# Eight experts' products in native float32 on four column tiles, with 96 token slots and a weight ring that is read as it lands

## The reference

```python
def moe_swiglu(v, router, wg, wu, wd):          # v: 256 x 1024
    logits = (v @ router).astype(F32)           # 8 experts
    top_val, top_idx = lax.top_k(logits, 2)
    top_w = jax.nn.softmax(top_val, axis=-1)
    combine = jnp.sum(jax.nn.one_hot(top_idx, 8, dtype=F32) * top_w[..., None], axis=-2)
    y = jnp.zeros_like(v)
    for e in range(8):                          # wg, wu: 1024 x 2816, wd: 2816 x 1024
        y = y + combine[..., e:e + 1] * swiglu(v, wg[e], wu[e], wd[e])
    return y
```

## Time and profile before

| | |
|---|---|
| time, median of 3 runs | 1569.23 us (1567.52 to 1570.71) |
| the profiled execution | 1568.84 us, its span 1567.1 us |
| PE, DVE, ACT busy | 99%, 80%, 64% of the span |
| the expert stage on PE | from 772.2 us to 1524.5 us, 48% of the span |
| DMA in the expert stage, from 1000 to 1100 us | 381 GB/s, busy share 1.03 |

### The profile page before, as it was taken

One profiled execution on the slowest core, in us unless ns is written; L12 is line 12 of the kernel. 1 busy time (PEld: TensorE's weight loads), 2 busy tenths in 40 slices (PEclk: granted clock), 3 DMA queues, 4 the chain that ended last, 5 costly groups with the idle time before them and its releaser, 6 DMA issues.

```text
span 1567.1 us, 20748 instructions
## 1 busy us (share of the span) xinstructions
PE 1548.3 (99%) x8098; PEld 1278.1 (82%) x8098; DVE 1253.5 (80%) x1438; ACT 999.7 (64%) x1219; POOL 63.4 (4%) x94
## 2 busy tenths in 40 slices
PE   8999999999999999999999999999999999999997
PEld 7887888888888888788878888888888888888876
DVE  5787878555566677788699999999999999999995
ACT  5656434544445556434578777777777877777774
POOL 3100000000000100000000000000000000001001
PEclk9999999999999999999999999999999999999999
DMA  8445445565555445452799999999999999999990
GB/s 294 136 146 176 147 151 195 177 197 188 185 194 161 151 153 169 145 169 98 280 371 384 385 384 373 385 377 385 384 374 387 370 386 379 386 377 376 395 355 28
DMA packets 212438, 421.31 MB, mean 269 GB/s; under 512 B 16194, under 2 KB 57972, under 8 KB 212340
## 3 DMA queue, kind: packets, MB, share of 16 engines
q1 hardware_dynamic: 207808, 407.69, 73.3%
q0 software_dynamic: 2880, 10.49, 1.7%
q10 hardware_dynamic: 1652, 1.80, 0.3%
HBM read 414.15 MB, written 5.77 MB: 268 GB/s over the span
## 4 chain that ended last, share of the span: by engine, by line
PE 95%; DVE 2%; ACT 1%; DMA 0%; POOL 0%; issue 0%; SPq 0%; POOLq 0%; DVEq 0%; ACTq 0%
PE ps L1518 29%; PE ps L1520 29%; PE ps L1519 29%; DVE wlo L939 1%; PE ps L1974 1%; PE ps L1617 1%; PE ps L1578 1%; PE ps L1764 1%; PE ps L1627 1%; DMA arena<-in_w_in 0%; PE ps L1943 0%; PE ps L1788 0%; ACT whi L587 0%; PE ps L1868 0%; PE ps L1749 0%
## 5 line engine op out<-in xcount | busy, mean ns | idle before, releaser
L939 DVE TENSOR_TENSOR wlo<-arena,whi 128x1024 fp32r<-128x1024 f32 x774 | 908.4, 1220 | 137.1 <-ACT whi L587 135.9
L587 ACT ACTIVATE whi<-arena 128x1024 fp32r<-128x1024 f32 x774 | 774.2, 1052 | 192.1 <-PE ps L1520 181.9
L1518 PE MATMUL ps<-whi,ahi 128*128 128x512 f32 (+1 forms) x2040 | 809.7, 397 | 4.2 <-DVE wlo L939 2.6
L1520 PE MATMUL ps<-wlo,ahi 128*128 128x512 f32 (+1 forms) x2040 | 796.0, 390 | 0.0
L1519 PE MATMUL ps<-whi,alo 128*128 128x512 f32 (+1 forms) x2040 | 794.7, 390 | 0.0
L1518 PEld LDWEIGHTS ps<-whi,ahi 128*128 128x128 f32 x2040 | 383.7, 188 | 85.3 <-issue 7.9
L1520 PEld LDWEIGHTS ps<-wlo,ahi 128*128 128x128 f32 x2040 | 383.3, 188 | 81.1
L1519 PEld LDWEIGHTS ps<-whi,alo 128*128 128x128 f32 x2040 | 384.2, 188 | 74.9
L939 DVE TENSOR_TENSOR alo<-ps,ahi 128x512 fp32r<-128x512 f32 (+2 forms) x93 | 62.5, 676 | 37.2 <-ACT ahi L587 34.8
L587 ACT ACTIVATE ahi<-ps 128x512 fp32r<-128x512 f32 (+2 forms) x46 | 27.3, 604 | 64.0 <-PE ps L1868 29.5
L716 ACT ACTIVATE ahi<-ps 128x512 fp32r<-128x512 f32 (+1 forms) x48 | 27.0, 563 | 49.8 <-PE ps L1974 49.8
(11 more groups left out here) (235 smaller groups left out, 721.2 us busy)
## 6 DMA issues: line engine op xcount, KB each, us to landing
arena<-in_moe_wg SPq DMA_DIRECT2D x176, 512.0 KB, 6.0
arena<-in_moe_wu SPq DMA_DIRECT2D x176, 512.0 KB, 6.4
arena<-in_moe_wd SPq DMA_DIRECT2D x176, 512.0 KB, 6.1
arena<-in_w_in SPq DMA_DIRECT2D x112, 512.0 KB, 4.5
arena<-in_w_branch SPq DMA_DIRECT2D x24, 512.0 KB, 4.5
arena<-in_dense_wg SPq DMA_DIRECT2D x22, 512.0 KB, 4.0
arena<-in_dense_wu SPq DMA_DIRECT2D x22, 512.0 KB, 5.0
arena<-in_dense_wd SPq DMA_DIRECT2D x22, 512.0 KB, 4.4
```

What stands on the lines that cost most here:

```text
L587: return nc.scalar.activation(dst, src, ACT.Copy)
L939: return V.tensor_tensor(dst, src, hi.bitcast(f32), ALU.subtract)
L1518: TE.matmul(o, ahi[:, sa], whi[:, sw], start=start, stop=False)
L1520: return TE.matmul(o, ahi[:, sa], wlo[:, sw], start=False, stop=stop)
```

## The change

The experts' products are done in plain float32, without any split. The stationary operand is 32 token slots of one 128-row chunk of the activations; the moving operand is the weights as they landed. Each block of 32 slots (`NB` = 3 blocks, `CAP` = 96 slots) is multiplied four times, each time with another quarter of the granule's columns, on another column tile: output rows 32i to 32i+31 of a bank hold the block's product with quarter i.

- `up_granule`: 4 chunks x 3 blocks x 4 tiles = 48 matmuls of 128 moving columns. `down_granule`: 2 x 3 x 4 = 24 matmuls of 256.
- No `convert` of expert granules on ACT and DVE. Silu, product and the copy of the transposes are 384 wide (192 for the last pair), one copy each on ACT (`ffT_out`), none on DVE.
- PE waits on the landing itself; a slot is free when PE is through with its granule (SP waits on `gemm_done`). There are seven slots, all in `arena` (`FREED`); `whi` and `wlo` stand idle until the PLE granules.
- Gathers fetch 96 rows. Stores to `y_rows` are four transfers with pieces of 1 KB. Expert 7 is scattered by 24 float32 matmuls with 32 rows of the array each (`combine_blocks`), with places that PE turned before.
- `overflow` now begins above 96 tokens.

```diff
+Q = 32
+NB = 3
+CAP = NB * Q
-RAW_MOE = 6
+ARENA_SLOTS = 7
+FREED = [4, 5, 6]
+for last in range(M0 - RAW, M0):
+    FREED += [last % RAW]
+SLOT_OF = [FREED[m % len(FREED)] for m in range(N_MOE)]
...
@@ sync
-            for m in range(N_MOE):
-                split(M0 + m - RAW_MOE)
+            for m in range(N_MOE + 5):
+                slot = SLOT_OF[m]
+                if BEFORE[m] is not None:
+                    sp.wait_ge(gemm_done, M0 + BEFORE[m] + 1)
...
@@ scalar
-            def ffT_hi(e, d):
-                nc.scalar.activation(ahi[:, FFT:FFT + w], bank(4, w), ACT.Copy).then_inc(m_thi, 1)
+            def ffT_out(e, d):
+                copy(wk(fft(d), pair_cols(d)), bank(4, pair_cols(d))).then_inc(m_fft, 1)
...
-                            convert(n + WR)
+                            if e == NE - 1 and k >= PER_E - WR:
+                                convert(n + WR)
...
@@ vector
-                            if kind in ("gate", "both") and part == 0 and j > 0:
-                                ffT_lo(e, j - 1)
...
-                            convert(n + WR)
...
@@ tensor
+                    def up_granule(n, q, part, out, both):
+                        pe.wait_ge(*landed_when(n))
+                        w = raw_of(n).rearrange("p (c s f) -> p c s f", c=4, s=2)
+                        for c in range(4):
+                            for b in range(NB):
+                                for i in range(4):
+                                    weights = w[:, c, :, 64 * i:64 * i + 64] if both else w[:, c, i // 2, P * (i % 2):P * (i % 2) + P]
+                                    o = bank(out, P, b * P)[tile_rows(i)]
+                                    last = TE.matmul(o.rearrange("p (s f) -> p s f", s=2) if both else o,
+                                                     wk(XG + (q * KC + 4 * part + c) * CAP + b * Q, Q), weights,
...
+                    def down_granule(n, j, split):
+                        pe.wait_ge(*landed_when(n))
...
+                            for i in range(4):
+                                ffT = b * P + (2 * (j % 2) + c) * Q if j < 2 * WIDE else b * 64 + c * Q
+                                last = TE.matmul(bank(2 + b // 2, FS, (b % 2) * FS)[tile_rows(i)], wk(fft(j // 2) + ffT, Q),
+                                                 w[:, c * D + i * FS:c * D + i * FS + FS],
...
```

More of the change, by code:

```diff
@@ L55, with pair_of @@
 N_MOE = NE * PER_E
+N_ALL = M0 + N_MOE + 5
+ARENA_SLOTS = 7
+def pair_of(ring):
+    return [ARENA_SLOTS + ring, ARENA_SLOTS + WR + ring]
+FREED = [4, 5, 6]
+for last in range(M0 - RAW, M0):
+    FREED += [last % RAW]
+SLOT_OF = [FREED[m % len(FREED)] for m in range(N_MOE)]
+for part in range(5):
+    waiting = [m for m in range(len(SLOT_OF)) if SLOT_OF[m] < ARENA_SLOTS and SLOT_OF[m] not in SLOT_OF[m + 1:]]
+    SLOT_OF.append(SLOT_OF[waiting[0]])
+BEFORE = [max([k for k in range(m) if SLOT_OF[k] == SLOT_OF[m]], default=None) for m in range(len(SLOT_OF))]
+USE = [sum(SLOT_OF[k] == SLOT_OF[m] for k in range(m)) for m in range(len(SLOT_OF))]
+RING_DONE = 0
+OVER_SLOT = [slot for slot in range(ARENA_SLOTS) if slot not in SLOT_OF[N_MOE:]][0]
 def build(nc, x, p, lb_param, norm_mix, w_in, hg_onorm, sa_cnorm, sa_wk, sa_wv, w_branch, w_out,
@@ L1413, in add_last_expert @@
                         V.memset(wk(GAP, 1), 0.0).then_inc(h_half, 2)
                     place_tokens(0, onehot)
-                    convert(base + G_OUT + 3 + WR)
-                    for half in range(2):
-                        xg_lo_of(0, half, half + 1)
+                    dve.wait_ge(gathered, 2)
+                    V.tensor_copy(x_half_of(0, 1).rearrange("p (c s) -> p c s", s=CAP),
+                                  bank(7).rearrange("p (c s) -> p c s", s=P)[:, :, 0:CAP]).then_inc(x_dve, 1)
@@ L1462, in _ @@
                                 lo_of_p()
-                            if kind == "down" and j in (6, 7) and e + 1 < NE:
-                                xg_lo_of(1 - q, j - 6, 2 * e + j - 6 + 3)
+                            if kind == "down" and j == 7 and e + 1 < NE:
+                                dve.wait_ge(gathered, 2 * e + 4)
+                                V.tensor_copy(x_half_of(1 - q, 1), bank(7, 4 * CAP)).then_inc(x_dve, 1)
                 first = base + G_PLE0 if layer == 0 else M0 + N_MOE
@@ L1954, in comb_transposed, with turn_spread @@
                         last.then_inc(done, 1)
-                    def combine_half(q, t, half, o):
-                        place, f = place_t[:, q * 256 + t * P:q * 256 + t * P + P], slice(half * 512, half * 512 + 512)
-                        TE.matmul(o, place, y_hi[:, f], start=True, stop=False)
-                        return TE.matmul(o, place, y_lo_[:, f], start=False, stop=True)
+                    def turn_spread(t):
+                        for b in range(NB):
+                            last = TE.transpose(bank(5, P, b * P), wk(SPREAD + (t * NB + b) * P, P), ident[:, :])
+                        last.then_inc(ct_done, 1)
@@ new lines, in combine_blocks @@
+                    def combine_blocks(some):
+                        for b in some:
+                            for t in range(NT):
+                                for i in range(4):
+                                    place = wk(XG + (t * NB + b) * P, P)[tile_rows(i)]
+                                    last = TE.matmul(bank(LAST_BANKS[i], FS, t * FS), place, wk(Y + b * FS, FS)[tile_rows(i)],
+                                                     start=b == 0 and t == 0, stop=b == NB - 1, skip_group_check=True)
+                        return last
```

346 lines of the change are left out of this document (189 added, 157 removed).

## The result

The change makes the kernel slower by 9%: 1713.62 us, median of 4 runs (1705.37 to 1718.15), against 1568.49 for the kernel before in the same session; the ratio is 1.0917, with a 95% interval of 1.0871 to 1.0963. The forecast was 1550 us, with a range of 1540 to 1578. The profiled execution of after took 1705.37 us and its span is 1703.6. The expert stage on PE grew from 752.3 us to 891 (770.5 to 1661.4), which is more than the whole difference of the spans, 136.5 us.

The account below looks back on a forecast made before the run. PE, full of its own work, was taken as the bound: eight experts of 91.6 us plus 0.9 make a stage of 733.7, 18.6 less, 19.2 with the end, so 1549.6, stated as 1550 us; range 1540 to 1578.

Parts of the forecast that it names:

- What bounds the kernel before: Expert stage: PE is full of its own work, 93.93 us an expert; removing the splitting by itself gives nothing.
- Rates of the new products: Expert products on PE: up granule 2.63 us, down granule 2.60, against 2.72 before for each.
- The rival of rates: Up granules: rounds of 128 columns take longer than 0.109 us; slower from 4.6 ns more, 1621 with 17 ns; chance 0.13.
- The sum for an expert: PE's work for one expert in the stage: 91.6 us, 2.3 less than before; ends 89.6 and 100.6.
- Waits and ends of the stage: Around expert products: other engines and slots do not hold PE; the stage's start stays, its end takes 0.6 us less.
- instruction fetches sit on one DMA engine: Expert stage: 21.6 packets an expert crowd one DMA engine, so granules land late; 1629 us in all; chance 0.09.
- The rival of the issue floor: Up granules: 17 ns a matmul record, 3.2 us per granule, about 1650 us; a quarter of a chance of 0.13.
- DMA as a bound: Transfers of the expert stage: 35.7 MB an expert at 395 GB/s take 90.4 us, 1% below PE's 91.6.
- DMA takes over: Expert stage: at only 381 GB/s transfers take 93.7 us an expert and PE waits; 1556 to 1560 us; chance 0.13.
- The signs: Token casts 91.6 us apart and equal mean PE bound; uneven, with PE idle and the landing named, mean DMA.

Follow-up runs that it names:

- e1_thin: The changed kernel, transferring only the first 1/32 of each expert weight row behind each slot's first granule; 1557.32 us, ratio 0.9919 to the kernel before.
- e8_bank5thin: e7_bank5 with weights left out as in e1_thin; 1545.97 us, ratio 0.9849 to the kernel before.
- e11_spread13: e10_spread with the weights in a ring of 13 slots, six added from the idle split buffers; 1559.81 us, ratio 0.9930 to the kernel before.
- e10_spread: e7_bank5 with the half pair's two granules cut into eight pieces laid between granules of 256 columns; 1681.34 us, ratio 1.0715 to the kernel before.
- e7_bank5: e3_pair with the products of each expert's last half pair in accumulation bank 5; 1560.93 us, ratio 0.9941 to the kernel before.
- e9_apart: e7_bank5 with the half pair's two granules moved apart, each between granules of 256 columns; 1559.51 us, ratio 0.9930 to the kernel before.
- e12_bank5_13: e7_bank5 with the weights in a ring of 13 slots; 1557.22 us, ratio 0.9921 to the kernel before.
- e3_pair: The changed kernel with gate and up columns together in one granule, so a matmul streams 256 columns; 1565.22 us, ratio 0.9972 to the kernel before.
- e5_up64: The changed kernel with gate and up matmuls of 64 columns in place of 128, twice as many; 2162.27 us, ratio 1.3776 to the kernel before.
- e6_up64thin: e5_up64 with weights left out as in e1_thin; 1953.95 us, ratio 1.2448 to the kernel before.
- e4_dn128: The changed kernel with down matmuls of 128 columns in place of 256, twice as many; 1791.57 us, ratio 1.1411 to the kernel before.
- e2_half: The changed kernel, transferring only half of each expert weight row behind each slot's first granule; 1574.84 us, ratio 1.0032 to the kernel before.

## Why the prediction was wrong

**What bounds the kernel before**: right. PE was full; the splitting cost nothing.

**Rates of the new products**: right to 1%. An up granule without a pause took 2.620 us at the least and 2.644 in the median (predicted 2.63), a round of four recorded matmuls 0.109; a down granule took 2.590 (predicted 2.60). One remark on it was wrong and changed nothing: at 2.4 GHz the row's 0.217 us fit 2 x 256 cycles (0.213), not 4 x 256 (0.427). The rival of rates, four tiles behind their rate, did not come about; the Trainium skill's factor of 2.38 for three tiles (TensorE: Matmul & The Clock Gate, Part 3, Measured speedup) has no match in this trace, where four kept the rates of rows 7 and 9. The sum for an expert, 91.6 us, was right to 1% for PE's work: 92.4 in e1_thin, with after's own order and hardly a pause; with wider matmuls 91.15 in e8_bank5thin and 90.87 in e11_spread13.

**Waits and ends of the stage**: right as far as they can be seen: PE waits for none of ACT, DVE or SP to speak of.

**The step that failed** is the one on instructions. It stands in the rival "instruction fetches sit on one DMA engine", and in the sum by its absence. I had counted the packets well: 21.6 an expert and about 210 in all, where 20.9 and 206 came. And I priced them only by the room that they take on DMA engines, 0.9 us an expert. What I did not ask is when the next packet arrives, for an engine that uses one up every 91.6 / 21.6 = 4.2 us, and every 3.5 in up granules. The price of that is 19 to 20 us an expert: 111.3 on average over six experts in place of 91.6. No row of before shows a fetch's duration, since its blocks last 29 us and hide it; the nearest I had was the stretch at L1764, 128 records, half a block. A count that rises six times, of something whose latency no row gives, should have been a rival with its own place in the range: with the 3.6 to 6.4 us that the runs now show, for each of 132 blocks of 3.5, that is a loss between 13 and 380 us. What the rival did describe, granules that land late because one DMA engine is crowded, did not come about: PE waits for no landing in after, and DMA moved less than before. Whether the packets sit on one engine the runs don't tell.

The rival of the issue floor came from the same section of the Trainium skill (Runtime: NRT & Kernel Launch, Instruction fetch mechanics). That section also says that fetches are hidden by the floor of about 20 cycles an instruction. Here 256 instructions were through in 3.5 us, 13.7 ns each, and a fetch took 3.6 us even beside idle transfers: once the engine is faster than the floor, the hiding ends, and the measurement decides. That this rival's time (1650) lies on the same side as the result is luck: its mechanism, a slower issue of every instruction, did not occur.

**DMA as a bound**: mis-sized. I took 395 GB/s and so 90.4 us an expert, 1% below PE. The stage moves 379 to 387 in e11_spread13, where no fetch holds it; 35.7 MB at 383 are 93.2 us. The two stretches at 394 and 396 were short. Without late fetches the rival "DMA takes over" would perhaps have been the result: its time was 1556 to 1560, and e11_spread13, the one version beside the spoiled e10_spread in which PE waits for landings and not for fetches, took 1559.81. That e7_bank5, e9_apart and e12_bank5_13 end there too, at 1557 to 1561, says nothing for it, since what holds them is pauses.

**The signs** I had named showed it at once: casts uneven, PE idle before products, with "issue" where a landing would stand for DMA. The 111.3 us of an expert are 92.4 plus the long pauses (142 us / 8 = 17.8) and about 1 us more, which the stretches at the lower clock can account for (at most 12 / 8 = 1.5).

## What to carry to other kernels

When a change multiplies the instructions of an engine, divide the time of a stretch by its instructions: 256 of them must last longer than a fetch, here 3.6 us beside idle transfers and 6.25 beside saturated ones, or the engine pauses for the rest, here at every 128th recorded matmul. Idle time with the releaser "issue", in the middle of loops, at equal counts of records, is the mark of it. The cure is wider matmuls for the same columns (here gate and up columns in one). It took back what the change had cost and 0.3% more (e3_pair), 0.6% with bank 5 (e7_bank5), and then the next bound, lying 1% away, takes what is left.

## What the runs showed of the hardware

- An instruction packet of 16.4 KB for TensorE takes 2.4 to 2.5 us from its start to the first use of its instructions (medians of after, e5_up64, e6_up64thin, e7_bank5, e9_apart); the start comes 1.1 to 1.7 us after the pause before it beside transfers of about 20 GB/s (e6_up64thin), 1.2 to 4.0 at 320 GB/s (after), and nearly always 3.8 at 383 (e7_bank5). That the request is made when the block before is entered, and only one block ahead, is inferred from these times and not shown directly.
- Four column tiles with 128 x 32 stationary operands and different moving streams take 0.109 us for four recorded matmuls of 128 columns (after, e1_thin) and 0.216 for 256 (e3_pair, beside 378 to 381 GB/s of landing weights); a float32 matmul of the program is two of these records.
- Half of the weights' bytes (195 to 198 GB/s) took off nearly all of the pauses: 15.5 of 139.4 us were left.
- The clock fell to its lower level (1.2 GHz) for stretches of mostly 3.4 us, up to 13.7, in stages with many or long idle times of PE: 24 us in all in after, 55 in e4_dn128, 102 in e10_spread, 276 in e5_up64; in e11_spread13 it fell at 1278.2 and at 1466.0 us, within idle times of PE of over 3 us. It stayed at the upper level (2.4 GHz) through the stages of before, e1_thin, e2_half, e3_pair and e7_bank5. So starving PE cost a second time, though little in after.
- Not tried: whether an engine without column tiles can be starved alike.
